# A transformer kernel's output projection: five split weight blocks kept for the second pass, the last norm's spread placed between the first FFN blocks, and one of its sums moved to GpSimd

## The reference, cut to what matters

```python
for layer in range(2):
    ...                                     # modulation, norm, projections, retention, attention, delta net
    y = concat([ret, swa, gdn]) @ w_out[layer]
    x = x + g1 * y
    h = rmsnorm(x, norm_ffn_w[layer]) * (1.0 + sc2) + sh2
    gu = h @ w_ffn_in[layer]
    x = x + g2 * ((silu(gu[..., :D_FF]) * gu[..., D_FF:]) @ w_ffn_out[layer])
return rmsnorm(x, final_norm_w)
```

## Time and profile before

| | |
|---|---|
| median of 3 runs | 3723.64 us (3721.9 to 3729.55) |
| profiled execution, its own time | 3734.98 us |
| span in its trace | 3733.2 us |
| TensorE busy | 3327.0 us (89% of the span) |
| DVE busy | 1644.3 us (44%) |
| ACT busy | 1060.6 us (28%) |
| GpSimd busy | 667.8 us (18%) |
| mean granted TensorE clock | 0.931 of full speed |

### The profile page before, as it was taken

How to read it: one execution, slowest core, us unless ns; L and a number is a source line. 1 busy time by engine, 2 the same in 40 slices (tenths; PEclk the granted TensorE clock), 3 DMA queues, 4 the chain that set the end, 5 groups by cost and what they waited for, 6 DMA issues and landing times. The chain is left out here.

```text
span 3733.2 us, 56373 instructions
## 1 busy us (share of the span) xinstructions
PE 3327.0 (89%) x21762; PEld 2792.9 (75%) x21762; DVE 1644.3 (44%) x2735; ACT 1060.6 (28%) x1934; POOL 667.8 (18%) x762
## 2 busy tenths in 40 slices
PE   4989856977899999999999999757887999999998
PEld 2878745866778888888887788646775778888886
DVE  5365776632453322223136465775633532322234
ACT  3344134612232121121213244134512331122112
POOL 1232763222000000000001132762222000000000
PEclk7999967988999999999999999868997999999998
DMA  4456185086521111111112465285194311111111
GB/s 175 150 190 202 62 282 157 18 233 183 196 64 40 35 39 40 39 39 34 39 40 83 139 194 189 74 281 149 38 263 168 110 42 51 47 49 51 45 51 62
DMA packets 245240, 405.31 MB, mean 109 GB/s; under 512 B 76083, under 2 KB 146483, under 8 KB 244662
## 3 DMA queue, kind: packets, MB, share of 16 engines
q1 hardware_dynamic: 239222, 382.76, 32.9%
q0 software_dynamic: 5824, 19.93, 1.4%
HBM read 289.97 MB, written 100.56 MB: 105 GB/s over the span
## 5 line engine op out<-in xcount | busy, mean ns | idle before, releaser
L924 DVE TENSOR_TENSOR ffn_w_lo<-ffn_raw,ffn_w_hi 128x1024 fp32r<-128x1024 f32 x164 | 200.8, 1225 | 500.6 <-ACT ffn_w_hi L920 495.4
L849 PE MATMUL frt_acc<-frt_w_hi,frt_h_hi 128*128 128x472 f32 x928 | 364.7, 393 | 51.2 <-DVE frt_w_lo L728 26.5
L930 PE MATMUL ffn_bank<-yr_hi,ffn_w_hi 128*128 128x512 f32 (+1 forms) x1040 | 386.3, 371 | 24.9 <-DVE ffn_w_lo L924 22.0
L930 PE MATMUL ffn_bank<-o_ys_hi,ffn_w_hi 128*128 128x512 f32 (+1 forms) x1040 | 387.2, 372 | 7.1 <-DVE o_ys_lo L1014 6.1
L933 PE MATMUL ffn_bank<-o_ys_lo,ffn_w_hi 128*128 128x512 f32 (+1 forms) x1040 | 384.7, 370 | 0.0
L934 PE MATMUL ffn_bank<-o_ys_hi,ffn_w_lo 128*128 128x512 f32 (+1 forms) x1040 | 384.1, 369 | 0.0
L933 PE MATMUL ffn_bank<-yr_lo,ffn_w_hi 128*128 128x512 f32 (+1 forms) x1040 | 384.0, 369 | 0.0
L934 PE MATMUL ffn_bank<-yr_hi,ffn_w_lo 128*128 128x512 f32 (+1 forms) x1040 | 383.9, 369 | 0.0
L849 PE MATMUL frt_acc<-frt_w_hi,frt_h_lo 128*128 128x472 f32 x928 | 355.8, 383 | 0.0
L849 PE MATMUL frt_acc<-frt_w_lo,frt_h_hi 128*128 128x472 f32 x928 | 355.1, 383 | 0.0
L930 PE MATMUL ffn_bank<-ffn_a_hi,ffn_w_hi 128*128 128x512 f32 (+1 forms) x880 | 324.3, 368 | 0.8 <-DVE ffn_a_lo L1191 0.8
(11 more groups left out here) (359 smaller groups left out, 5785.9 us busy)
## 6 DMA issues: line engine op xcount, KB each, us to landing
ffn_raw<-w_ffn SPq DMA_DIRECT2D x132, 512.0 KB, 3.6
x<-ada_w SPq DMA_DIRECT2D x15, 2048.0 KB, 9.2
proj<-frt_out SPq DMA_DIRECT2D x116, 236.0 KB, 2.0
x<-proj SPq DMA_DIRECT2D x60, 384.0 KB, 4.6
frt_raw<-w_in SPq DMA_DIRECT2D x96, 236.0 KB, 4.3
ffn_raw<-w_out SPq DMA_DIRECT2D x32, 512.0 KB, 3.7
met_pr<-proj SPq DMA_DIRECT2D x20, 768.0 KB, 6.5
met_vn<-pack SPq DMA_DIRECT2D x20, 640.0 KB, 6.3
```

What stands on the lines that cost most here:

```text
L849: mm = pe.matmul(acc[q % NA][:, 0:GW], a[:, k, tok], b[:, k, :], start=(k == 0 and i == 0), stop=(k == KC - 1 and i == 2))
L924: dve.tensor_tensor(self.lo[u][:], self.raw[u][:], self.hi[u][:].bitcast(F32), ALU.subtract).then_inc(self.ready[u], 1)
L930: mm = pe.matmul(out, w_hi, b_hi, start=first, stop=False)
```

## The change

- **Weights.** Nine loads for each layer instead of 16 (`splits`). Splits 0 to 4 go into `a_hi` and `a_lo` and stay there; 5, 6 and 7 go into the two ordinary slots (5 in slot 0, 6 in slot 1, 7 in slot 0 again), and block 5 is loaded and split a second time at the end (split 8, slot 1). The second pass runs over the blocks in the order 7, 6, 0, 1, 2, 3, 4, 5 (`second`): 7 and 6 are still in the ordinary slots, 0 to 4 are the kept ones.
- **Order on ACT and DVE in the second pass.** All early norm steps of a unit now stand ahead of any weight split, and ACT rounds the unit's first step ahead of its square. ACT takes the early root directly behind the square of unit 8; before, a weight rounding stood between. The first two FFN blocks' weights are split in unit 12 and behind unit 15.
- **Squares of the late slice.** GpSimd adds them up (seven additions of 128 x 512 for each layer), no longer DVE.
- **Late norm.** `pe_sums` stands inside block 0 of the last early slice, behind k = 4, and `pe_spread` ahead of block 1 early instead of behind it.

```diff
-        passes = [(i, i % MU, i // MU) for i in range(2 * MU)]
+        kept = a_hi[:].rearrange("p j n -> p (j n)"), a_lo[:].rearrange("p j n -> p (j n)")
+        KEEP = 5
+        splits = [0, 1, 2, 3, 4, 5, 6, 7, 5]
...
+        stored = lambda n: [kept[i][:, n * DM:(n + 1) * DM] if n < KEEP else (w.hi, w.lo)[i][1 if n in (6, 8) else 0][:] for i in range(2)]
+        passes = [(i, m, 0) for i, m in enumerate(range(KC))] + [(KC + i, m, 1) for i, m in enumerate(second)]
+        split_of = list(range(KC)) + [7, 6, 0, 1, 2, 3, 4, 8]
...
+        def act_split(act, n):
+            if n < 7:
+                act.wait_ge(m_landed[n % 2], n // 2 * 16 + 16)
+                act.activation(stored(n)[0], w.raw[1 - n % 2][:], ACT.Copy).then_inc(m_rounded, 1)
+            elif n == 7:
+                act.wait_ge(m_begun, 7)
+                w.round(act, 0, 0, True)
+            else:
+                act.wait_ge(m_begun, KC + 3)
+                w.round(act, 1, 0, True)
...
+        def splits_beside(i):
+
+            if i < 6:
+                return [i + 2]
+            return {KC + 2: [8]}.get(i, [])
...
         def dve_mix(dve):
-            for u in range(2):
-                w.rest(dve, u, 0)
+            for n in range(2):
+                dve_split(dve, n)
             for i, m, g in passes:
-                steps = early_steps(m) if g == 1 else []
-                dve_add(dve, m, g)
-                if steps:
-                    norm.dve_step(dve, 0, steps[0])
-                for j in range(len(group[g])):
-                    sq_mix[g].gather(dve, m, j)
-                w.rest(dve, i % 2, i // 2 + 1)
-                if g == 1 and m == 0:
+                q = i % KC
+                steps = early_steps(q) if g == 1 else []
+                if g == 0:
+                    for n in splits_beside(i):
+                        dve_split(dve, n)
+                dve_add(dve, i, m, g)
+                for step in steps:
+                    norm.dve_step(dve, 0, step)
+                if g == 0:
+                    for j in range(len(group[g])):
+                        sq_mix[g].gather(dve, q, j)
+                if g == 1 and q == 0:
                     norm.dve_lay(dve, 0)
-                for step in steps[1:]:
-                    norm.dve_step(dve, 0, step)
+                if g == 1:
+                    for n in splits_beside(i):
+                        dve_split(dve, n)
+                if i == KC + 4:
+                    w.rest(dve, 0, 1)
+            w.rest(dve, 1, 1)
             norm.dve_lay(dve, 1)
...
+                    if summing and k == 4:
+                        norm.pe_sums(pe, 1, sq_mix[1].gathered, gathers[1])
...
             for s in early_s:
-                unit(0, s)
-            norm.pe_sums(pe, 1, sq_mix[1].gathered, gathers[1])
+                unit(0, s, s == early_s[-1])
+            norm.pe_spread(pe, 1, free[1], MB)
             for s in early_s:
                 unit(1, s)
-            norm.pe_spread(pe, 1, free[1], MB)
             for s in late_s:
...
-                for i, m, g in passes:
-                    if i >= 2:
-                        sp.wait_ge(w.ready[i % 2], i // 2)
-                    sp.dma_start(w.raw[i % 2][:], w_out[m]).then_inc(w.landed[i % 2], 16)
+                for n, m in enumerate(splits):
+                    if n >= 2:
+                        sp.wait_ge(m_ready, n - 1)
+                    sp.dma_start(w.raw[1 - n % 2][:], w_out[m]).then_inc(w.landed[n - 7] if n >= 7 else m_landed[n % 2], 16)
...
+                for q in range(KC):
+                    if q >= 2:
+                        pool.wait_ge(sq_mix[1].gathered, q - 1)
+                    sq_mix[1].gather(pool, q, 0)
```

More of the change, by code:

```diff
@@ L1062, in mixed_ffn, with early_steps @@
+        passes = [(i, m, 0) for i, m in enumerate(range(KC))] + [(KC + i, m, 1) for i, m in enumerate(second)]
+        split_of = list(range(KC)) + [7, 6, 0, 1, 2, 3, 4, 8]
         group = [early_s, late_s]
-        gathers = [(MU - 1) * len(g) for g in group]
+        gathers = [(KC - 1) * len(g) for g in group]
         spots = [2, 3, 3, 2, 2, 2, 2] if NS == 3 else [1, 1, 1, 1, 1, 1, 2]
-        def early_steps(m):
-            done = sum(spots[:max(m - 1, 0)])
-            return list(norm.steps(0))[done:done + (spots[m - 1] if m else 0)]
+        def early_steps(q):
+            done = sum(spots[:max(q - 1, 0)])
+            return list(norm.steps(0))[done:done + (spots[q - 1] if q else 0)]
@@ L1101, in act_mix @@
             for i, m, g in passes:
-                for j, s in enumerate(group[g]):
-                    act.wait_ge(free[m % 2][s], m // 2 + 1)
-                    sq_mix[g].square(act, m, j)
-                w.round(act, i % 2, i // 2 + 1)
-                if g == 1:
-                    if m == 0:
-                        norm.act_root(act, 0)
-                    for step in early_steps(m):
-                        norm.act_round(act, step)
+                q = i % KC
+                steps = early_steps(q) if g == 1 else []
@@ new lines, in act_mix @@
+                if g == 0:
+                    for n in splits_beside(i):
+                        act_split(act, n)
+                for step in steps[:1]:
+                    norm.act_round(act, step)
+                for j, s in enumerate(group[g]):
+                    act.wait_ge(free[q % 2][s], q // 2 + 1)
+                    sq_mix[g].square(act, q, j)
+                if g == 1 and q == 0:
+                    norm.act_root(act, 0)
+                for step in steps[1:]:
+                    norm.act_round(act, step)
@@ L1136, in pe_first, with unit @@
         def pe_first(pe):
-            def unit(u, s):
+            def unit(u, s, summing=False):
                 t0, ln = slices[s]
```

71 lines of the change are left out of this document (50 added, 21 removed).

## The result

The changed kernel took 3695.71 us (median of 5 runs, 3681.58 to 3704.28) against 3722.53 us for the kernel before in the same job (median of 5, 3721.9 to 3729.55). The ratio is 0.9917, with a 95% interval of 0.9889 to 0.9945: faster by 20 to 41 us. I had forecast 3700, from a sum of 23.9 us. The ratio, put on the median of before, gives 3692.7, which is 0.3 us beyond the low end of my range; so the question is whether the change gave more than I had counted, or something else did.

A forecast was written before the change was run, and what follows sets the result against it. TensorE, busy 89% of the span, was taken as the bound, so only its waits or slowdowns mattered. 6.9 + 3.0 + 1.7 + 7.3 + 5.46 - 0.5 = 23.9 us off 3723.6 gave 3700, range 3693 to 3713.

The forecast's parts named there:

- Part 1, the four weight waits: Second mixing pass: TensorE's four waits for `lo` weights in layer 0 go, and layer 1's short ones; with the root, 6.9 and 3.0 us.
- Part 2 and 3, the root and the last early step: Second pass: the root's wait (1.08) goes in both layers; layer 1's block 0 early: the last early step's wait, 1.7 with restart.
- Part 4, the spread ahead of block 1 early: FFN start: block 1 early runs while the late norm's steps run, giving 7.3 us in layer 0 and 5.46 in layer 1.
- Part 5, collisions: Late sums and spread: inputs in time, but GpSimd and DVE meetings may delay them, 0 to 1.5 us for both layers, 0.5 taken.
- The signs: No second-pass weight or early-spread waits; layer 0's late spread about 10.2 us behind unit 15; layer 1 13.8 from spread to end.
- one sign of being wrong: TensorE waits at the late sums behind k = 4; other such signs: spread waiting for layout, FFN clock below 0.95 and 0.88.
- The rivals: Across both stretches: gain cut by new waits (15%, 3712), waits hid nothing lost (6%, 3717 to 3724), slower through DVE collisions (4%, 3729).
- New waits and a lower clock: Block 0 late: late steps start later or the clock falls, cutting the gain to 12 us, 3712; chance 15%.
- 4 us for the spread of the runs: Whole-kernel time: allowance for scatter of the timed runs, used in setting the range 3693 to 3713.
- the main case: Whole kernel: a gain of 19 to 28 us, so 3696 to 3705 us, with a 75% chance.

## Why the prediction was right, and where it was wrong

- **What bounds the kernel.** Right. All that the change gave came from TensorE's waits and half-speed stretches at the two places.
- **Part 1, the four weight waits.** They went, but the cause that I gave for them failed. I wrote "The cause is the length of a unit" and that the weights "stand in line behind the addition, a norm step, the square and the gather", added up busy time, and took the removal of the splits as the cure. That is a cure (10.7 us by itself), but not the one that was needed. DVE was not short of time: it stood idle 1.3 to 1.7 us in each of the seven units of layer 0 that have norm steps, waiting for one rounding that ACT had placed behind its square and a weight rounding. Moving that rounding gave 9.3, the whole new order 11.9, and the kept weights 0.6 on top. The group for DVE's rests (L1014, 3.2 us idle for ACT's `yr_hi`) shows the wait that I did not follow up.
- **Part 2 and 3, the root and the last early step.** Right in kind and nearly in size: parts 1 to 3 were 11.6 in my sum and measured 12.6.
- **Part 4, the spread ahead of block 1 early.** Right: 7.3 and 5.46 in the sum. Measured on top of the new order it was 7.4 (74.17 to 66.73) and 5.2 (67.52 to 62.34), with GpSimd's loss in it; without GpSimd 7.4 and 5.4 (74.77 to 67.37, 67.54 to 62.10). The 13.77 us from spread to end stayed in layer 1, and its waits stood in the later k.
- **Part 5, collisions.** Right in kind. I took 0.5 of a possible 1.5; GpSimd's part costs 0.26. Single meetings cost as much as I had put down, or more: the gather lost 0.62 us (I had 0.45), the second rest 0.82 and, with GpSimd's work doubled, the split 1.07 (I had 0.84). Ten of the fourteen gathers took 1.65 us or more, over my 1.0 to 1.5.
- **The signs.** The second passes and the late spread came as written: TensorE has no wait there, the spread of layer 0 starts 9.27 us behind the end of unit 15 and ends about 10.2 behind it, and block 0 late has no wait in layer 0. The sums of layer 1 were 0.15 us late, a first trace of one sign of being wrong, without an idle row.
- **The rivals.** New waits and a lower clock did not come, and the clock in the FFN stretches went to 1.00. The doubled GpSimd work shows how near this was in layer 1: a wait of 1.4 cost 3.0.
- **How the numbers follow.** The sum was right to 1.3 us: 23.9, and the profile has 25.2. Of the 1.3 us between them 1.0 is in parts 1 to 3, 0.1 in part 4 and 0.2 in the allowance of part 5. Taken off the 3723.6 from which I reckoned, 25.2 us give 3698.4, well inside the range. The term that failed is the last one, "4 us for the spread of the runs": the first ratio alone has an interval of 10 us to either side, and the two ratios of the same kernel, 0.9917 and 0.9950, are 12 us apart, on both sides of the 0.9932 that the stretches give. My own arithmetic was short as well, as the low end, 3693, is 3 us and not 4 under the 3696 of the main case; the 3692.7 lies between the two. That the outcome missed the range by 0.3 us rather than hit it is luck, as a hit would have been.
- **What is scatter.** The profiled difference of spans, 30.8, is 25.2 of the change and 5.6 of what lies outside the stretches, which took 3561 to 3579 us in fourteen executions. It moves ahead of the mixing of each layer, also between kernels whose code is the same up to there (965.8 to 977.2 us). The five runs of the changed kernel spread over 23 us. That the first ratio's excess is such scatter is consistent with all this and not proved run by run, since a profile shows one execution only. What makes the part ahead of the mixing take longer or shorter was not tried.

## What to carry to other kernels

When an engine's result is late, follow the idle time in front of it before adding up its work: here an engine busy for two thirds of the time was late because it waited 1.6 us for an instruction that another engine could have run earlier, and moving that one instruction gave 9.3 us, where fourteen saved loads and splits gave 10.7. Where a norm's chain of small steps must run before the next matmuls, put its start ahead of a block that does not need it; what counts is whether that block is as long as the chain. Judge parts of a few us by the same stretch of several profiles, since the rest of the program moved by up to 18 us between executions.

## What the runs showed of the hardware

- The length of a single wait did not decide whether TensorE's clock fell. A wait of 1.13 us (late norm moved alone) and one of 1.40 us (GpSimd's work doubled) were each followed by matmuls at half the clock: the granted clock was 0.50 from 2972.00 to 2974.20 in the one, and nine matmuls took 3.7 us instead of 2.2 in the other. The waits of 0.88 to 1.72 us in the second pass of layer 0 in the kernel before, and the one of 1.44 in layer 1, were not: the granted clock there is 1.00. The longest of them and its window:

```profile
1085.56 0.50 PE L930 MATMUL ffn_bank<-yr_hi,ffn_w_hi 128*128 128x512 f32 x1 [1.72 <-DVE ffn_w_lo L924]
...
1085.00:1092.00 7.00, 5.74 (x24) 4.43 (x24) 5.39 (x8) 2.81 (x4) 0.00 (x0) 1.00 0.21 75
```

  What does decide it, these runs do not show. The price of such a wait was a little more than itself (1.14 for 0.88 in the prediction) or more than double (3.0 for 1.40).
- A DVE instruction and a GpSimd instruction that both read two arrays of SBUF delayed each other: 1.67 for 1.04 us on GpSimd; 1.57 for 0.75 on DVE's rest and 2.28 for 1.21 on its split.
